# A hybrid decoder step on one core: scan order, stage ends, x1 tile by tile and transposed sample rows, in one change

## The reference, cut to what matters

```
for x in (x_prompt 1x256x2048, x_sample 8x8x2048, with past states):     # 320 tokens in all
  p   = RMSNorm(x) @ W_in                       # z | xBC | dt | glu
  xBC = silu(conv4(xBC)); y = SSD scan (32 heads, 4 groups, state 128, chunks of 128) + D * x
  ssd = group RMSNorm(y * silu(z))
  cf  = silu(LayerNorm(conv31(glu_a * sigmoid(glu_b))))
  x   = x + RMSNorm([ssd, cf] @ W_out)          # "x1"
  x   = x + RMSNorm(relu(RMSNorm(x) @ W_up)**2 @ W_down)     # D_FF = 8192
outputs: x of prompt and samples, new scan states and convolution states
```

## Time and profile before

| | |
|---|---|
| median of 3 runs | 1827.09 us (1825.63 to 1829.25) |
| the profiled execution | 1823.92 us, span 1822.3 |
| PE busy | 1793.7 us, 98% |
| DVE / ACT / POOL busy | 1088.4 / 769.9 / 457.4 us |
| granted TensorE clock, mean | 0.993 |
| DMA | 278 MB, 153 GB/s over the span |
| chain that ended last | PE 95%, DVE 2%, ACT 1%, issue 1% |

### The profile page before, as it was taken

One profiled execution on the slowest core, in us unless ns is written; L12 is line 12 of the kernel. 1 busy time (PEld: TensorE's weight loads), 2 busy tenths in 40 slices (PEclk: granted clock), 3 DMA queues, 4 the chain that ended last, 5 costly groups with the idle time before them and its releaser, 6 DMA issues.

```text
span 1822.3 us, 33899 instructions
## 1 busy us (share of the span) xinstructions
PE 1793.7 (98%) x12686; PEld 1758.8 (97%) x12686; DVE 1088.4 (60%) x1992; ACT 769.9 (42%) x1139; POOL 457.4 (25%) x351
## 2 busy tenths in 40 slices
PE   8999999999999999999899999999999999999998
PEld 7999999999998898899899999999999999999997
DVE  5587878999777677755675433444334434444444
ACT  6443435555365565532444333433334333333342
POOL 1577766677651122223000000000000000000121
PEclk9999999999998999999999999999999999999999
DMA  8665554555544555464354544445444454444442
GB/s 251 172 186 154 154 155 139 152 143 159 154 138 147 155 172 158 146 204 154 93 162 138 160 156 146 139 146 166 150 138 140 159 162 139 138 159 156 148 139 81
DMA packets 287283, 278.32 MB, mean 153 GB/s; under 512 B 11574, under 2 KB 284702, under 8 KB 286320
## 3 DMA queue, kind: packets, MB, share of 16 engines
q1 hardware_dynamic: 248376, 246.56, 44.3%
q10 hardware_dynamic: 37168, 23.08, 4.3%
q0 software_dynamic: 1648, 7.43, 1.3%
HBM read 261.25 MB, written 17.22 MB: 153 GB/s over the span
## 4 chain that ended last, share of the span: by engine, by line
PE 95%; DVE 2%; ACT 1%; issue 1%; DMA 0%; SPq 0%; DVEq 0%; ACTq 0%
PE ps L1778 28%; PE ps L1779 28%; PE ps L1780 28%; PE ps L2103 1%; PE ps L2105 1%; PE ps L2104 1%; PE ps L2064 1%; PE ps L2058 1%; PE ps L1835 1%; PE ps L2032 1%; PE ps L1837 1%; PE ps L1836 1%; PE ps L2009 1%; DMA xn<-in_x_prompt 0%; PE ps L2069 0%
## 5 line engine op out<-in xcount | busy, mean ns | idle before, releaser
L1778 PE MATMUL ps<-ahi,whi 128*128 128x320 f32 x2304 | 719.2, 312 | 1.9 <-DVE alo L1465 1.9
L1780 PE MATMUL ps<-ahi,wlo 128*128 128x320 f32 x2304 | 712.9, 309 | 0.0
L1779 PE MATMUL ps<-alo,whi 128*128 128x320 f32 x2304 | 712.9, 309 | 0.0
L666 ACT ACTIVATE whi<-raw 128x1024 fp32r<-128x1024 f32 (+1 forms) x467 | 479.1, 1048 | 466.7 <-PE ps L1780 386.7
L1197 DVE TENSOR_TENSOR wlo<-raw,whi 128x1024 fp32r<-128x1024 f32 x346 | 424.1, 1250 | 245.8 <-ACT whi L666 242.7
L1778 PEld LDWEIGHTS ps<-ahi,whi 128*128 128x128 f32 x2304 | 433.7, 188 | 4.0 <-DVE alo L1465 2.2
L1779 PEld LDWEIGHTS ps<-alo,whi 128*128 128x128 f32 x2304 | 433.7, 188 | 0.5
L1780 PEld LDWEIGHTS ps<-ahi,wlo 128*128 128x128 f32 x2304 | 433.4, 188 | 0.0
L1778 PE MATMUL ps<-hhi,whi 128*128 128x320 f32 x1016 | 314.3, 309 | 0.0
L500 POOL TENSOR_TENSOR wlo<-raw,whi 128x1024 fp32r<-128x1024 f32 x121 | 289.8, 2417 | 96.9 <-ACT whi L666 96.5
L1780 PE MATMUL ps<-hhi,wlo 128*128 128x320 f32 x1016 | 313.9, 309 | 0.0
(11 more groups left out here) (304 smaller groups left out, 1645.5 us busy)
## 6 DMA issues: line engine op xcount, KB each, us to landing
raw<-in_w_in SPq DMA_DIRECT2D x144, 512.0 KB, 3.7
raw<-in_w_up SPq DMA_DIRECT2D x128, 512.0 KB, 4.3
raw<-in_w_down SPq DMA_DIRECT2D x128, 512.0 KB, 4.4
raw<-in_w_out SPq DMA_DIRECT2D x64, 512.0 KB, 3.5
h<-in_state_ssm ACTq DMA_DIRECT2D x16, 512.0 KB, 5.3
out<-hout ACTq DMA_DIRECT2D x16, 512.0 KB, 3.3
x_transposed<-xt ACTq DMA_DIRECT2D x1, 2560.0 KB, 10.2
xr<-x_transposed POOLq DMA_DIRECT2D x1, 2560.0 KB, 9.7
```

Of the source, the lines that this page charges most:

```text
L666: act.activation(whi[:, kq, :, 0:width], raw[:, kq, :, 0:width], ACT.Copy).then_inc(hi_done, 1)
L1778: pe.matmul(out, wh, hi[:, kk, :], start=(kk == 0), stop=False)
L1779: pe.matmul(out, wh, lo[:, kk, :], start=False, stop=False)
L1780: last = pe.matmul(out, wl, hi[:, kk, :], start=False, stop=(kk == NT - 1))
```

## The change

1. LayerNorm into the scan: one weight split goes from GpSimd to VectorE; the first part's silu and cast stand before the normalization of parts 2 and 3; the silu of part 3 (ScalarE) and the casts of parts 2 and 3 (VectorE) stand inside turn 0, behind the copy of B's rows; `bm` is made behind the first mask. GpSimd starts on `selt` after half of the activations.
2. Each turn: `hts` is copied before the second decay; the 32 small state products stand behind `st_done`.
3. Ws's first turn: new order, three splits ahead of the gate's root, `diag` before the two sums. `xr` is scaled by the norm during Ws's turns 1 and 2 (`scale_x`), so that x1 needs no `q1s`. The last turn is unrolled on TensorE, and tile 14 of mix is released by itself.
4. x1: GpSimd folds its two sums to one; nine wide matmuls on old data into bank 7 behind the statistics; each x1 tile is used for both pairs and in all quarters as soon as it is there (12 matmuls a tile); x1's parts are made tile by tile; VectorE's last splits stand between the sums of squares; `rms_x1` stands behind the second quarter of pair 2.
5. End: tile 14's squares are added on VectorE, the column sums take two rounds, ten output blocks in the order of `OUT_BLOCKS`, sample rows of two column groups in one block on partitions 0 to 63 and 64 to 127 (made by plain matmuls), three reciprocals where first needed, outputs issued from SyncE (token rows 0 to 127 and half of the samples) and ScalarE (the rest), one transfer a block or half block.

```
-WS_FIRST = ((0, 0), (0, 1), (0, 2), (1, 0), (1, 1), (1, 2), (0, 3), (1, 3))
+WS_FIRST = ((0, 0), (0, 1), (1, 0), (1, 1), (0, 2), (1, 2), (0, 3), (1, 3))
...
+OUT_BLOCKS = ((0, 0), (0, 1), (1, 0), (1, 1), (0, 2), (2, 0), (2, 1), (3, 0), (3, 1), (2, 2))
...
     pool.sem_inc(msum_done, 1)
-    for c in (1, 2, 3, 5, 6, 7):
+    for c in (1, 2, 3, 5, 6):
...
         st.leave(7)
-    pool.sem_inc(acc_done, 1)
+    pool.tensor_tensor(acc2[:, 0, :], acc2[:, 0, :], acc2[:, 1, :], ALU.add).then_inc(acc_done, 1)
...
         if c == 6:
             z_silu(3, 0)
-            conf_silu(0)
+    conf_silu(0)
     conf_silu(1)
+    z_silu(3, 1)
     conf_silu(2)
...
                                ).then_inc(btok_ready, 1)
-            if not first:
+            if first:
+                conf_silu(3)
+            else:
                 act.wait_ge(y_done, T)
             decay(T, 0)
             act.wait_ge(h0_trans, T + 1)
...
                 act.wait_ge(y_read, T)
             act.activation(ecb[:], ps[:, 2, TOK:512], ACT.Copy).then_inc(ecb_ready, 1)
-            decay(T, 1)
             act.wait_ge(pstart_done, T + 1)
             act.activation(hts[:], ps[:, 4, 384:512], ACT.Copy).then_inc(hts_ready, 1)
+            decay(T, 1)
             if j % 2:
                 p = j // 2
...
-            ahead(Q_MLP, 0, 4)
-            ahead(Q_MLP, 0, 5)
+    for t in range(NT):
+        act.wait_ge(xp_done, t + 1)
+        act.activation(ahi[:, t, :], mix[:, t, :], ACT.Copy, scale=par[:, t, R_PREMLP:R_PREMLP + 1]
+                       ).then_inc(ahi_done, 1)
+        if t % 4 == 3:
+            square_x1(t // 4)
+        if t in (5, 6, 9, 10):
+            ahead(Q_MLP, 0, {5: 2, 6: 3, 9: 4, 10: 5}[t])
     act.wait_ge(hout_out, 16 * NT)
...
-    for gg in range(3):
-        normalize(gg)
+    normalize(0)
+    normalize(1)
+    ahead(Q_Z, 3, 7)
     conf_act(0)
+    normalize(2)
     normalize(3)
-    for gg in range(1, 4):
-        conf_act(gg)
+    conf_act(1)
...
-            ahead(Q_WC, i, 2 * j)
-            if j == 0:
-                dve.wait_ge(btok_ready, i + 1)
...
                 dve.wait_ge(cb_masked, i + 1)
+            if first:
+                conf_act(2)
             dve.wait_ge(exp_done, 2 * T + 1)
             dve.tensor_tensor(wgt[:, 0, :], cb, wgt[:, 0, :], ALU.mult).then_inc(mixw_done, 1)
+            if j == 0:
+                dve.wait_ge(btok_ready, i + 1)
+                if not first:
+                    dve.wait_ge(st_done, 4 * i)
...
-            ahead(Q_WC, i, 2 * j + 1)
+            ahead(Q_WC, i, 0 if first else 2 * j + 1)
...
+                conf_act(3)
+                ahead(Q_WC, i, 1)
             dve.wait_ge(st_done, T + 1)
...
         ahead(Q_WS, 0, 0)
         gate_lo(2)
-        ahead(Q_WS, 0, 1)
+        for c in range(1, 4):
+            ahead(Q_WS, 0, c)
         gate_scale(3)
-        ahead(Q_WS, 0, 2)
         gate_mult(3)
-        ahead(Q_WS, 0, 3)
+        ahead(Q_WS, 0, 4)
...
+        for c in range(5, 8):
             ahead(Q_WS, 0, c)
+        dve.wait_ge(hout_out, 16 * NT)
+        for c in range(3):
+            last = dve.tensor_scalar(diag[:, c, :], ident[:], sx[:, c:c + 1], None, ALU.mult)
+        last.then_inc(sdiag_done, 1)
         for p in range(2):
             dve.wait_ge(weights_used, 4 * Q_WS + 7 + p)
             m = mix[:, 2 * p:2 * p + 2, :]
             dve.tensor_tensor(m, gemm_bank(p), m, ALU.add).then_inc(read_dve, 1)
             dve.tensor_tensor(m, gemm_bank(p), m, ALU.add).then_inc(read_dve, 1)
-    def ws(i, last=False):
+    def scale_x(g):
+        x = xr[:, 4 * g:4 * g + 4, :]
+        dve.tensor_tensor(x, x, ps[:, 5, 0:TOK].unsqueeze(1).to_broadcast([P, 4, TOK]), ALU.mult
+                          ).then_inc(q1s_done, 1)
+    def ws(i, last=False, scale_from=None):
         for c in range(8):
             ahead(Q_WS, i, c)
+            if scale_from is not None and c in (1, 5):
+                scale_x(scale_from + c // 4)
...
     first_ws()
-    dve.wait_ge(hout_out, 16 * NT)
-    for c in range(3):
-        last = dve.tensor_scalar(diag[:, c, :], ident[:], sx[:, c:c + 1], None, ALU.mult)
-    last.then_inc(sdiag_done, 1)
-    with dve.Fori(1, 3) as i:
-        ws(i)
+    dve.wait_ge(xr_in, 16)
+    dve.wait_ge(s_mm, 1)
+    for i in range(1, 3):
+        ws(i, scale_from=2 * (i - 1))
     ws(3, last=True)
...
-    for g in range(4):
-        if g == 0:
-            dve.wait_ge(s_mm, 1)
-            dve.tensor_tensor(q1s[:], ps[:, 5, 0:TOK], q1[:], ALU.mult).then_inc(q1s_done, 1)
-            dve.wait_ge(q1s_done, 1)
-        else:
...
-            ahead(Q_MLP, 0, 1)
-        elif g > 1:
-            ahead(Q_MLP, 0, 2 * g - 2)
-            ahead(Q_MLP, 0, 2 * g - 1)
+    def x1_part(t):
+        if t >= 4:
+            dve.wait_ge(xp_done, t - 3)
+        dve.tensor_tensor(t4[:, t % 4, :], xr[:, t, :], q1[:], ALU.mult).then_inc(t4_done, 1)
+    def x1_sum(t):
+        dve.wait_ge(t4_done, t + 1)
+        dve.scalar_tensor_tensor(out=mix[:, t, :], in0=mix[:, t, :],
+                                 scalar=par[:, t, R_POSTMIX:R_POSTMIX + 1], in1=t4[:, t % 4, :],
+                                 op0=ALU.mult, op1=ALU.add).then_inc(xp_done, 1)
+    dve.wait_ge(q1s_done, 4)
+    x1_part(0)
+    x1_sum(0)
+    x1_part(1)
+    x1_lo(0)
+    x1_sum(1)
+    for t in range(2, NT):
+        x1_part(t)
+        x1_sum(t)
+        x1_lo(t - 1)
+        if t in (4, 7, 8, 11, 12):
+            ahead(Q_MLP, 0, {4: 1, 7: 2, 8: 3, 11: 4, 12: 5}[t])
+    x1_lo(NT - 1)
     for g in range(1, 4):
+        ahead(Q_MLP, 0, 5 + g)
         dve.wait_ge(sqx_done, g + 1)
         if g > 1:
             dve.wait_ge(dve_step, v)
         v = st.inc(dve.tensor_tensor(sqx[:, 0:4, :], sqx[:, 0:4, :], sqx[:, 4 * g:4 * g + 4, :], ALU.add))
     dve.wait_ge(dve_step, v)
     dve.sem_inc(acc_done, 1)
-    for c in range(6, 10):
-        ahead(Q_MLP, 0, c)
+    ahead(Q_MLP, 0, 9)
     v = st.inc(dve.tensor_tensor(qq[:], q1[:], q1[:], ALU.mult))
...
                         m = ya[:, NT - 2 + n, :]
                         dve.tensor_tensor(m, ps[:, 2 + n, 0:TOK], m, ALU.add).then_inc(last_added, 1)
+                        if n == 0:
+                            dve.wait_ge(acc_done, 3)
+                            dve.wait_ge(sqm_done, 3)
+                            dve.tensor_tensor(acc2[:, 0, :], acc2[:, 0, :], sqm[:, 0, :], ALU.add
+                                              ).then_inc(acc_sum, 1)
...
         pe.wait_ge(h0t_ready, T + 1)
-        for b in range(NB):
-            for e in range(2):
...
         last.then_inc(st_done, 1)
+        for b in range(NB):
+            for e in range(2):
...
             pe.wait_ge(read_act, 36)
+        if s == 2:
+            pe.wait_ge(mixw_done, 2 * NT)
+            pe.wait_ge(ecb_ready, NT)
         if s == 3:
             gate_mean(3)
-            pe.wait_ge(mixw_done, 2 * NT)
...
+    for p in range(2):
+        pe.wait_ge(read_dve, 8 + 6 + p - 1)
+        for kq in range(4):
+            granule(Q_WS + 6 + p, kq, 2 * p, ghi, glo, by_tile=mix_tile if p and kq == 3 else None)
     pe.wait_ge(acc_done, 1)
-    for n in range(2):
-        pe.matmul(ps[:, 4, 0:TOK], mean1[:], acc2[:, n, :], start=(n == 0), stop=False)
+    pe.matmul(ps[:, 4, 0:TOK], mean1[:], acc2[:, 0, :], start=True, stop=False)
     for n in range(2):
         pe.wait_ge(sqm_done, n + 1)
         last = pe.matmul(ps[:, 4, 0:TOK], mean1[:], sqm[:, n, :], start=False, stop=(n == 1))
     last.then_inc(rms_mm, 1)
+    pe.wait_ge(hnew_done, NT)
+    wide = ghi[:].rearrange("p t n -> p (t n)")[:, 0:512]
+    for _ in range(9):
+        pe.matmul(ps[:, 7, :], ghi[:, 15, 0:P], wide, start=True, stop=True)
+    def up0(q, counts):
+        gemm(q_up(q), 0, ahi, alo, counts)
...
-    for s in range(8):
-        kq, p = s // 2, s % 2
-        if kq == 0:
-            pe.wait_ge(read_dve, 15 + p)
-        if p == 0:
-            pe.wait_ge(act_ready, 2 * NT + 4 * kq + 1)
-        piece(4 * Q_MLP + s, s % 4, kq, 2 * p, ahi, alo, first=(p == 0))
-    rms_x1()
+    pe.wait_ge(read_dve, 16)
     for kq in range(4):
+        for p in range(2):
+            slot = 2 * (kq % 2) + p
+            pe.wait_ge(lo_done[slot], Q_MLP + kq // 2 + 1)
+        for k in range(4):
+            kk = 4 * kq + k
+            pe.wait_ge(act_ready, 2 * NT + kk + 1)
+            for p in range(2):
+                slot = 2 * (kq % 2) + p
+                for n in range(2):
+                    wh, wl = whi[:, slot, k, n * P:(n + 1) * P], wlo[:, slot, k, n * P:(n + 1) * P]
+                    out = ps[:, 2 * p + n, 0:TOK]
+                    pe.matmul(out, wh, ahi[:, kk, :], start=(kk == 0), stop=False)
+                    pe.matmul(out, wh, alo[:, kk, :], start=False, stop=False)
+                    last = pe.matmul(out, wl, ahi[:, kk, :], start=False, stop=(kk == NT - 1))
+                if k == 3:
+                    last.then_inc(weights_used, 1)
+    for kq in range(4):
+        if kq == 2:
```

(28 more changed lines are left out.)

146 lines of the change are left out of this document (65 added, 81 removed).

## The result

| | before | after |
|---|---|---|
| median | 1827.39 us (1825.59 to 1829.25, 6 runs) | 1809.82 us (1809.73 to 1810.76, 6 runs) |
| profiled execution, its span | 1823.92, 1822.3 | 1809.74, 1808.1 |
| granted clock, mean | 0.993 | 0.998 |

The ratio is 0.9906, its 95% interval 0.9894 to 0.9918. The spans differ by 14.2. The other 3.4 us is new: the median of before lies 3.5 above its profiled execution, that of after 0.1.

The account below looks back on a forecast made before the run. TensorE was taken as the bound, with gains only where it waits or runs at half clock. 3.5 + 0.9 + 3.0 - 2.5 + 3.2 = 8.1 us took the median from 1827.09 to 1819.0, range 1813.5 to 1823.7.

Parts of the forecast that it names:

- part 2: Scan turns with a gate: copying `hts` before the second decay gains 0.3 us in each of three turns, 0.9 in all.
- part 1: LayerNorm into the scan: removing the 1.90 us wait and half clock, less new waits in the first turns, gains 3.5 us.
- part 3: First output columns of Ws: the waits for `glo`, a weight split and `diag` go, gaining 3.0 us.
- part 5: The end: fewer column-sum rounds, ten output blocks instead of twelve and two output queues gain 3.2 us.
- part 4: x1 and up: pair 3 starts 0.7 us later after a 4 us wait, with 1.8 of half clock: loss 2.5 us.
- I put the same difference under it: Base time: the median before lies 3.2 us above the profiled execution, and the changed kernel's median was given the same difference.
- moved, not removed; in other turns nothing waits there: Scan turns without a gate: moving the 32 small state products changes nothing, and the turn stays at 12.72 us.
- Loss after: 4.7 of 8.2: Scan turns 0 and 1: after the change 3.5 us of waits and 1.2 of half clock remain of 8.2 lost.
- The 8.2: Scan turns 0 and 1: they took 34.8 us where 26.5 would do, so 8.2 us were lost.
- Rival A: Pair 3 doesn't stall: its first split comes sooner, the first turns lose no clock, gain 14.2 us, 1812.9; chance 0.12.
- B: Rival: scan's first turns keep their loss because deferred work only moves the wait; gain 3.4 us, 1823.7; chance 0.22.
- C: Rival: the clock stays at half through scan turns 0 and 1, making the kernel slower, 1832 us; chance 0.04.

Follow-up runs that it names:

- a_prod: The changed kernel with the 32 small state products put back ahead of the wait for `bm`: median 1811.08 us.
- b_hts: The kernel before with `hts` copied ahead of the second decay and nothing else: median 1822.16 us.
- b_same: The kernel before run again without an edit: twelve executions, median 1824.22 us.

## Why the prediction was right and wrong

**The miss, by steps.** The median was missed by 9.2 us. The terms that made it up are 3.1 in the base, 2.7 in part 2, 2.35 in part 1, 0.5 in part 3, 0.4 in part 5 and 0.1 in part 4. The steps that failed are "I put the same difference under it", "moved, not removed; in other turns nothing waits there", and "Loss after: 4.7 of 8.2"; what the runs showed in their place stands below.

**Bound and direction**: right. The 855 us did not move, and the gain is in waits and half clock, but for the 0.1 us a turn that the order of the small products gives and the shorter end.

**Part 1** (3.5 forecast, 5.85): right in the mechanism, mis-sized in what is left over. Of "0.8 btok, 1.1 masks, 1.6 pst, 1.2 of clock" the profile shows 0.51, 0.55, 1.08 and 0, that is 2.1 for 4.7. The 8.2 were measured rightly but named only in part: beside the 1.90 and the 1.6 the prediction did not see the 1.45 us wait for the first mask and the 7.5 us at a granted clock of 0.54 behind it, which were more than half of them. The reason given for the short cast was half of it: the overlap was the cause, but moving the split was not what took it away.

**Part 2** (0.9, 3.62): the step that failed is "moved, not removed; in other turns nothing waits". The 0.3 per gated turn is right to 0.02. Missing are 0.10 us in each turn without a gate (1.3 in the median of `a_prod`) and the 1.53 of half clock behind a wait of 0.74. From the 1.5 us wait for `diag` I had taken the clock to stay up behind so short a wait; the wait of 1.45 in turn 0 of the same trace, with half clock behind it, speaks against that. Nor did I see that the one move alone would have cost 20 us.

**Part 3** (3.0, 3.53): right in the stretch, but the wait of 0.8 for `glo` was not its to remove; undone alone it costs 2.4.

**Part 4** (-2.5, -2.42): right, with its chain: from the EPS sum at 917.91 to the first split's end at 928.8 it is 10.9 us again, the wait 4.14 for 4, the half clock 1.57 for 1.8. The nine wide products were put at nothing, and as long as pair 3 waits, the traces bear that out; with pair 3 mended they are worth 1.3. Of the half clock behind the 4 us wait the size is partly luck: ten profiled executions have a wait of 4.14 there, and from pair 3 to the last product they lose 1.4 to 2.8 us against the 863.97 of before. Rival A's time was nearest (1812.9), by a mechanism that did not occur. B and C fell: the leftover in turns 0 and 1 was 2.1 us, all at full clock. Of the rule behind C, that transposes do not count as activity (the Trainium skill's page "TensorE: Matmul & The Clock Gate", Part 4: PE-mode transpose), no run shows an effect: turns with 11 and with 14 transposes ran at a clock of 1.00.

**Part 5** (3.2, 3.62): right; the sample blocks took 1.51 us, between the two bounds.

**The base**: "I put the same difference under it" failed: 3.2 us was put under the profiled execution, 0.1 was measured, and that is 3.1 of the 9.2 us. A part of the 3.2 was the sample of three, since the 84 executions of before have their median 2.2 above the profiled one. The rest belonged to half clock that comes in some executions and not in others, behind waits that the change removes.

## What to carry to other kernels

If a kernel's executions spread by several us and its clock with them, price every short wait of TensorE twice: its length, and the half clock that it brings in a part of the executions. Then compare clocks window by window before you give an edit what one profiled execution gained. Before moving small work, ask what it hides; the products that seemed to be free cargo were the cover of a copy. And where one stage is made faster, look for the next operand that is prepared only behind the old end of that stage: here two splits in other places were worth 5.3 us, and made a gain of a stage that had lost 1.8.

## What the runs showed of the hardware

A wait of 0.74 us for `hts` led to half clock in some executions and not in others, and each time it did, it cost 1.5. The one of 1.90 ahead of the scan did in five profiled executions and not in that of `b_hts`. The one of 1.50 for `diag` took no half clock along in any of seven, nor did one of 1.6 for `pst` in `a_prod`, while the one of 1.45 for the first mask had it behind it in before and `b_same`, in turns where the clock had already been down 10 us earlier. Those of 3.0, 3.8 and 4.1 always did, and behind the same 4.14 us the loss went from 1.4 to 2.8 us. That is no order by length alone, and what else decides it stays open. A VectorE pass under a GpSimd subtraction of 2.4 us ended up to 2.3 us later, the subtraction itself no later, if the pass did not read `ps`; passes that read `ps` kept their length. The same 32 small products took 1.03 us ahead of one group of products and 0.95 behind another.
